# Gates of a product-key expert layer: summed and scattered into DRAM arrays instead of built by one-hot matmuls

## The chip, the cores and the metric

The kernel runs on one core of one Trainium2 chip. The metric is the device time of one execution in microseconds (us); smaller is better. TensorE is called PE, VectorE DVE, ScalarE ACT, GpSimd POOL and SyncE SP, as in the profile.

## What is computed

One decoder layer over T = 256 tokens of D = 2048. A mixing block (two projections, two causal convolutions, layer norm) gives x1; then every token chooses experts by product keys:

```python
q = (x_tok @ w_q).reshape(t, PEER_HEADS, 2, D_HALF)          # 8 heads
s = jnp.einsum('thpc,hpnc->thpn', q, sub_keys)               # 2 x 128 scores a head
s1, i1 = lax.top_k(s[:, :, 0], 16);  s2, i2 = lax.top_k(s[:, :, 1], 16)
cand = (s1[..., :, None] + s2[..., None, :]).reshape(t, 8, 256)
top_s, ci = lax.top_k(cand, 16)
experts = e1 * N_KEYS + e2                                   # e1, e2 looked up by ci; 16384 experts
g = jax.nn.softmax(top_s, axis=-1)
act = jax.nn.gelu(jnp.einsum('td,thkd->thk', x_tok, peer_u[experts]))
out = jnp.einsum('thk,thkd->td', act * g, peer_v[experts])
x = layer_norm(ALPHA * x + out)
```

Each token has 8 x 16 = 128 selections (expert, gate); two heads may select the same expert, and then their gates add.

## The kernel before

The kernel does not gather experts for most tokens. It multiplies x1 with all 16384 rows of `peer_u` and then all of `peer_v`, and weights the activations by a gate matrix that is zero where a token did not select the expert. 192 of the 256 tokens (`TD`) go this dense way. For the last 64 tokens (`SPARSE`) the activations are stored to DRAM, and the selected rows of `peer_v` are gathered by indirect DMAs and added on DVE (`pick`).

**Units.** All weights stream through as units of 128 x 1024 f32 (512 KB): SP loads a unit into one of 4 `raw` slots (`load`, which waits until the low part of the unit 4 before it is made), ACT rounds it into a high part (`hi`, line 638, which waits until PE has finished the unit 4 before it), DVE subtracts to get a low part (`lo`, line 876), and PE multiplies with 3 products per block: high by high, high by low, low by high (lines 1470 to 1472). Of the units from `U_Q` to `U_ROUTED`, POOL makes the low part (line 563) because DVE is busy with the routing (top-k, decoding the chosen indices). Between these loads SP also copies `peer_v` into a layout with whole rows (`copy_unit`, `v_rows`).

**Up stage.** Tile c (0 to 127) holds the activations of 128 experts for 256 tokens: 2 units, 48 matmuls of 256 columns into bank c % 2. ACT applies gelu when the tile is done and writes tokens 0 to 191 into `hid[:, c, :]` and the other 64 into `stage`. In this text unit n of the up stage is `U_UP + n`; tile c is units 2c and 2c + 1. The engines run in the order in which their code is written, so a wait holds everything behind it on its engine. ACT's and DVE's loops over c do, in turn, the high and low part of units a little ahead of the tile, and whatever the stage adds.

**Gates.** When the selections are ready (`sel`: first index, second index, gate; line 1211), PE transposes them (`transpose_selections`, in tile `SEL_AT` = 13). From tile 16 on, every third tile, the gates of 8 tokens are made (`gate_batch`): DVE builds two one-hot tiles (lines 1243 to 1259), PE multiplies them in 8 matmuls of 256 columns in 16-bit types (line 1606) between the two units of a tile, ACT and DVE put the result (high and low part) into `hid` and `gtmp` and fold it into the activations already there. There are 24 batches; the last stands in tile 85. Later tiles are multiplied as they come (`gate_tile_of`, line 1279).

**Down stage.** `coef_hi` and `coef_lo` split 4 tiles of `hid` (a group g, 32 groups) into operands, and PE multiplies them with the units of `peer_v`. Then comes the last layer norm.

## Time and profile before

| | |
|---|---|
| median of 3 runs | 1789.7 us (1789.25 to 1790.16) |
| profiled execution | 1791.2 us |
| its span, first to last instruction | 1789.4 us |
| mean granted TensorE clock | 0.996 |
| PE, PE weight load, DVE, ACT, POOL busy | 98%, 90%, 75%, 48%, 26% |
| DMA | 534.5 MB moved, 299 GB/s |

A busy PE is not a PE at its peak: matmuls overlap, so their durations (about 280 ns each in the up stage) say little, and the distance from one start to the next says what one costs. Idle time of the other engines matters only where PE waits at the end of it.

### The profile page before, as it was taken

To read this page: it belongs to the slowest core of one execution; us is meant where nothing else is said; L and a number is where in the kernel's file an instruction comes from. 1 tells how busy PE (TensorE), PEld (TensorE's weight loads), DVE (VectorE), ACT (ScalarE), POOL (GpSimd) and SP (SyncE) were. 2 spreads that over 40 slices of the span, in tenths; PEclk is the share of its full clock that TensorE was granted. 3 is DMA by queue.
4 is the path that set the end of the run, shared out by engine and by line. 5 is a ranking of instruction groups with operands and counts; after the bars stand their busy time and mean duration, and the time that the engine had idled before them with its cause. 6 is when DMAs were issued, how large, how long until landed. Compare 5 with 4: busy or idle time off the path is not lost.

```text
span 1789.4 us, 31898 instructions
## 1 busy us (share of the span) xinstructions
PE 1761.0 (98%) x12082; PEld 1618.3 (90%) x12082; DVE 1338.9 (75%) x1897; ACT 853.5 (48%) x1208; POOL 467.1 (26%) x278
## 2 busy tenths in 40 slices
PE   7999999899999999999999999999999999999997
PEld 7999987799999999999999999988878788888875
DVE  7999997687847777777775444557888888888876
ACT  5544445444544444444444444444544445445544
POOL 0000000488850000000000000034568775454401
PEclk9999999999999999999999999999999999999999
DMA  7788878778888888878888888878999999999973
GB/s 265 283 306 292 290 271 292 276 275 269 290 285 282 278 274 277 281 266 281 276 274 290 292 288 292 294 231 310 366 382 374 387 384 377 358 368 350 344 254 119
DMA packets 184098, 534.50 MB, mean 299 GB/s; under 512 B 35344, under 2 KB 35472, under 8 KB 182416
## 3 DMA queue, kind: packets, MB, share of 16 engines
q1 hardware_dynamic: 149664, 460.64, 73.0%
q0 software_dynamic: 16464, 67.68, 10.0%
q10 hardware_dynamic: 17888, 5.26, 1.2%
q8 instruction: 30, 0.49, 0.1%
q14 instruction: 52, 0.43, 0.1%
HBM read 524.50 MB, written 109.05 MB: 354 GB/s over the span
## 4 chain that ended last, share of the span: by engine, by line
PE 95%; DVE 2%; issue 1%; DMA 1%; ACT 1%; DVEq 0%; POOLq 0%; POOL 0%; SPq 0%; ACTq 0%
PE psum L1470 19%; PE psum L1472 19%; PE psum L1471 19%; PE psum L1643 6%; PE psum L1639 6%; PE psum L1644 6%; PE psum L1641 6%; PE psum L1640 6%; PE psum L1606 1%; PE psum L1514 1%; PE psum L1516 1%; PE psum L1515 1%; DMA raw<-in_v_w_dram 1%; DVE w_lo L876 1%; PE psum L1554 0%
## 5 line engine op out<-in xcount | busy, mean ns | idle before, releaser
L638 ACT ACTIVATE w_hi<-raw 128x1024 fp32r<-128x1024 f32 x570 | 604.0, 1061 | 736.4 <-PE psum L1472 492.9
L1470 PE MATMUL psum<-xt_hi,w_hi 128*128 128x256 f32 x2944 | 827.5, 281 | 11.8 <-DVE xt_lo L890 9.4
L876 DVE TENSOR_TENSOR w_lo<-raw,w_hi 128x1024 fp32r<-128x1024 f32 x506 | 614.1, 1223 | 292.2 <-ACT w_hi L638 281.1
L1471 PE MATMUL psum<-xt_lo,w_hi 128*128 128x256 f32 x2944 | 823.7, 280 | 0.0
L1472 PE MATMUL psum<-xt_hi,w_lo 128*128 128x256 f32 x2944 | 823.5, 280 | 0.0
L1470 PEld LDWEIGHTS psum<-xt_hi,w_hi 128*128 128x128 f32 x2944 | 555.5, 189 | 12.4 <-issue 12.0
L1471 PEld LDWEIGHTS psum<-xt_lo,w_hi 128*128 128x128 f32 x2944 | 555.4, 189 | 0.0
L1472 PEld LDWEIGHTS psum<-xt_hi,w_lo 128*128 128x128 f32 x2944 | 555.3, 189 | 0.0
L586 POOL DMA_INDIRECT rows<-v_rows,sp_idx x64 | 112.2, 1754 | 767.8 <-DMA v_rows<-in_v_w_dram 621.1
L563 POOL TENSOR_TENSOR w_lo<-raw,w_hi 128x1024 fp32r<-128x1024 f32 x64 | 153.8, 2408 | 363.2 <-ACT w_hi L638 363.1
L1639 PE MATMUL psum<-w_hi,c_hi 128*128 128x512 f32 x504 | 199.6, 396 | 0.9 <-DVE w_lo L876 0.8
L1641 PE MATMUL psum<-w_hi,c_lo 128*128 128x512 f32 x504 | 199.3, 396 | 0.0
L1640 PE MATMUL psum<-w_lo,c_hi 128*128 128x512 f32 x504 | 199.3, 395 | 0.0
L1644 PE MATMUL psum<-w_lo,c_both 128*128 128x512 f32 x504 | 199.3, 395 | 0.0
L1643 PE MATMUL psum<-w_hi,c_both 128*128 128x512 f32 x504 | 199.3, 395 | 0.0
L1342 DVE SCALAR_TENSOR_TENSOR picked<-rows,sp_coef,picked 128x2048 f32<-128x2048 f32 x63 | 148.1, 2351 | 0.5 <-DMA rows<-in_v_w_dram,sp_idx 0.4
L638 ACT ACTIVATE w_hi<-raw_late 128x1024 fp32r<-128x1024 f32 x82 | 87.0, 1062 | 96.4 <-PE psum L1644 85.2
L1639 PEld LDWEIGHTS psum<-w_hi,c_hi 128*128 128x128 f32 x504 | 94.7, 188 | 25.1 <-DVE w_lo L876 2.2
L1643 PEld LDWEIGHTS psum<-w_hi,c_both 128*128 128x128 f32 x504 | 94.7, 188 | 23.1 <-DVE w_lo L876 0.2
L1641 PEld LDWEIGHTS psum<-w_hi,c_lo 128*128 128x128 f32 x504 | 94.7, 188 | 22.9
L1644 PEld LDWEIGHTS psum<-w_lo,c_both 128*128 128x128 f32 x504 | 94.7, 188 | 22.9
L1640 PEld LDWEIGHTS psum<-w_lo,c_hi 128*128 128x128 f32 x504 | 94.7, 188 | 22.6
(191 smaller groups left out, 1395.9 us busy)
## 6 DMA issues: line engine op xcount, KB each, us to landing
raw<-in_u_w_dram SPq DMA_DIRECT2D x256, 512.0 KB
v_rows<-in_v_w_dram SPq DMA_DIRECT2D x192, 512.0 KB, 5.3
raw<-in_v_w_dram SPq DMA_DIRECT2D x172, 512.0 KB
raw_late<-in_v_w_dram SPq DMA_DIRECT2D x84, 512.0 KB
raw<-in_w_in_dram SPq DMA_DIRECT2D x80, 512.0 KB
raw<-in_w_out_dram SPq DMA_DIRECT2D x32, 512.0 KB
raw<-in_w_q_dram SPq DMA_DIRECT2D x32, 512.0 KB
act_spill<-stage ACTq DMA_DIRECT2D x32, 128.0 KB, 4.4
```

The source lines that it names most:

```text
L563: nc.gpsimd.tensor_tensor(w_lo[s][:, :], raw[:, s, :], w_hi[s][:, :].bitcast(f32), ALU.subtract).then_inc(lo_done[s], SPLIT)
L638: nc.scalar.activation(parts_of(slot_u)[0][:, :], raw_of(slot_u), ACT.Copy).then_inc(hi_done, 1)
L876: tt(lo_w[:, :], raw_of(slot_u), hi_w[:, :].bitcast(f32), ALU.subtract).then_inc(lo_done[slot_u % SPLIT], SPLIT)
L1342: i = stt(picked[:, :], rows[k % ROWS][:, :], sp_coef[:, k:k + 1], picked[:, :], ALU.mult, ALU.add)
L1470: mm(dst, hi_w[:, sl], xt_hi[:, kk, :], start=st, stop=False)
L1471: mm(dst, hi_w[:, sl], xt_lo[:, kk, :], start=False, stop=False)
L1472: i = mm(dst, lo_w[:, sl], xt_hi[:, kk, :], start=False, stop=en)
L1639: mm(v_bank(j, 0), hi_c[:, n, :], w1, start=st, stop=False)
L1640: mm(v_bank(j, 0), hi_c[:, n, :], w2, start=False, stop=False)
L1641: i = mm(v_bank(j, 0), lo_c[:, n, :], w1, start=False, stop=en)
L1643: mm(v_bank(j, 1), both_c[:, n, :], w1, start=st, stop=False)
L1644: i = mm(v_bank(j, 1), both_c[:, n, :], w2, start=False, stop=en)
```

## The change

No one-hot tiles, no gate matmuls and no transposes of the selections. Instead:

- DVE computes an id (e1 * 128 + e2) for each selection and, for every selection of a token, the sum of the gates of all selections of that token with the same id (`merge`: compare, multiply, reduce over 128 x 8 x 128 elements at a time). `merge(0)` does tokens 0 to 127 in 16 rounds; `merge(1)` does tokens 128 to 191, spread over all 128 partitions, in 8 rounds. ACT issues the DMAs that lay the inputs and the results out (`SEL_AT` = 10, `RELAY0_AT` = 20, `RELAY1_AT` = 26).
- SP writes zeros into 6 DRAM arrays of 2 MB, 32 tokens each (`zeros`, 8 times 6 DMAs of 256 KB, units 16 to 72 of the whole stream).
- POOL scatters the sums into the arrays with 32 x 6 = 192 indirect DMAs of 128 elements of 4 bytes; each waits for the one before it on its array. Equal selections write equal sums.
- SP loads the gates of a group of 4 tiles with 6 DMAs of 64 KB (`gates`), the first before unit 195 of the up stage; DVE multiplies them into `hid` (`gate_group`), from its loop step c = `GATED_AT` = 95 on, ahead of the low part of unit 2c + 3.
- POOL makes 16 more low parts (`U_ROUTED` = `U_UP` + 48 instead of 32), and the copies of `peer_v` end 48 units sooner (`COPY1`).

The core of the diff ("..." where lines are left out):

```diff
-PART_OF_TILE = 6
+PART_OF_TILE = 2
-SEL_AT = 13
-U_ROUTED = U_UP + 32
-GATE0 = 16
-GATE_STEP = 3
+SEL_AT = 10
+ROUTED_AT = 30
+U_ROUTED = U_UP + 48
+GATED_AT = 95
+RELAY0_AT, RELAY1_AT = 20, 26
+SAME = 8
+TOKENS = 32
+ZEROED = 4
+ARRAYS = TD // TOKENS
+QUARTERS = P // TOKENS
+EACH = SELECTED // QUARTERS
+def gates_unit(g):
+    return U_UP + 2 * (GATED_AT + g - 2) + 9
-COPY0, COPY1 = 24, U_DOWN - 8
+COPY0, COPY1 = 24, U_UP + 200
...
@@ sync
+            def zeros(n):
+                if n == 0:
+                    sp.wait_ge(zero_made, 1)
+                for a in range(ARRAYS):
+                    sp.dma_start(gate_tiles[a][:, ZEROED * n:ZEROED * (n + 1), :],
+                                 g_buf[:, 0, 0:ZEROED].rearrange("p g k t -> p g (k t)")).then_inc(zero_out, 16)
+            def gates(g):
+                if g == 0:
+                    for done in scattered:
+                        sp.wait_ge(done, 16 * EACH)
+                if g >= 2:
+                    sp.wait_ge(gated_done, g - 1)
+                for a in range(ARRAYS):
+                    sp.dma_start(g_buf[:, g % 2, a].rearrange("p k t -> p (k t)"), gate_tiles[a][:, g, :])\
+                        .then_inc(g_in[g % 2], 16)
             def stream(src, base, first, end):
                 for n in range(first, end):
                     u = base + n
+                    if 16 <= u < 16 + 8 * GROUPS // ZEROED and u % 8 == 0:
+                        zeros((u - 16) // 8)
+                    for g in range(GROUPS):
+                        if u == gates_unit(g):
+                            gates(g)
                     load(u, src[n])
...
@@ gpsimd
+            pool.wait_ge(zero_out, 16 * ARRAYS * GROUPS // ZEROED)
+            pool.wait_ge(relaid, 16 * ARRAYS * QUARTERS)
+            for k in range(EACH):
+                for a in range(ARRAYS):
+                    if k:
+                        pool.wait_ge(scattered[a], 16 * k)
+                    nc.gpsimd.indirect_dma_start(
+                        gate_array[a], bass.IndirectOffsetOnAxis(sc[:, a, 1, k:k + 1].bitcast(u32), 0),
+                        sc[:, a, 0, k:k + 1], None).then_inc(scattered[a], 16)
...
@@ scalar
-            def gates_out(m):
...
+                if c == RELAY0_AT:
+                    act.wait_ge(scat_ready, 1)
+                    for a in range(P // TOKENS):
+                        for q in range(QUARTERS):
+                            act.dma_start(sc[TOKENS * q:TOKENS * (q + 1), a, :, :],
+                                          sums[0][TOKENS * a:TOKENS * (a + 1), :, EACH * q:EACH * (q + 1)])\
+                                .then_inc(relaid, 16)
+                if c == RELAY1_AT:
+                    act.wait_ge(scat_ready, 2)
...
@@ vector
+            def merge(part, own, everyone, gates, n):
+                link_dup(nc.vector.tensor_copy(all_ids[part], everyone))
+                dve.wait_ge(dup, n_dup[0])
+                link_dup(ts(place_f[part][:, :], own, float(TOKENS), tok[:, 1:2], ALU.mult, ALU.add))
+                dve.wait_ge(dup, n_dup[0])
+                link_dup(nc.vector.tensor_copy(sums[part][:, 1, :].bitcast(u32), place_f[part][:, :]))
+                def matches(m):
+                    link_dup(tt(same[m % 2], own[:, SAME * m:SAME * (m + 1)].unsqueeze(2).to_broadcast([P, SAME, SELECTED]),
+                                all_ids[part].unsqueeze(1).to_broadcast([P, SAME, SELECTED]), ALU.is_equal))
+                matches(0)
+                for m in range(n // SAME):
+                    dve.wait_ge(dup, n_dup[0])
+                    link_dup(tt(same[m % 2], same[m % 2], gates.unsqueeze(1).to_broadcast([P, SAME, SELECTED]), ALU.mult))
+                    product = n_dup[0]
+                    if m + 1 < n // SAME:
+                        matches(m + 1)
+                    dve.wait_ge(dup, product)
+                    i = nc.vector.tensor_reduce(sums[part][:, 0, SAME * m:SAME * (m + 1)], same[m % 2], AX.X, ALU.add)
...
+            def gate_group(g):
+                dve.wait_ge(gelu_done, PART_OF_TILE * GROUP * (g + 1))
+                dve.wait_ge(g_in[g % 2], 16 * ARRAYS * (g // 2 + 1))
+                mine = hid[:, GROUP * g:GROUP * (g + 1), :].rearrange("p k (a t) -> p a k t", a=ARRAYS)
+                tt(mine, mine, g_buf[:, g % 2], ALU.mult).then_inc(gated_done, 1)
...
             for c in range((U_ROUTED - LEAD - U_UP) // 2, N_KEYS):
                 u = U_UP + 2 * c + LEAD
+                if c >= GATED_AT and c - GATED_AT < GROUPS - 1:
+                    gate_group(c - GATED_AT)
+                for v in (u, u + 1):
+                    if v >= U_ROUTED:
+                        lo(v, v)
...
@@ tensor
-            def gate_batch(m):
-                pe.wait_ge(oh1_done, m + 1)
-                pe.wait_ge(oh2_done, PARTS * m + PARTS)
...
-                for t in range(BATCH):
-                    i = mm(bank[2 + t // 2][:, (t % 2) * PARTS * N_KEYS:(t % 2 + 1) * PARTS * N_KEYS], oh1[:, t // INNER, :, t % INNER],
-                           oh2g[:, t // INNER, :, :, t % INNER].rearrange("p w e -> p (w e)"), start=True, stop=True)
-                i.then_inc(g_done, 1)
```

On DVE, behind the last instruction of the routing (it makes the gates in `sel`), the kernel before goes on with PE's transposes and the first one-hots, and then with the low parts:

```order
L1211 TENSOR_TENSOR sel<-sel,ssum 128x256 [waits rt]
L1214 CAST tab<-psum 128x256 [waits sel_tr]
L1216 TENSOR_SCALAR gate_e<-gate 128x256 [waits tabs_copied]
...
L1243 TENSOR_TENSOR oh<-iota_t,tab 128x1024 [waits tabs_copied,tabs_done]
L1245 TENSOR_TENSOR oh<-oh,gate_p 128x1024 [waits oh1_eq]
L1251 TENSOR_TENSOR oh2g<-iota_t,tab 128x4x256
L1259 TENSOR_TENSOR oh2g<-oh2g,gate_t 128x4x256 [waits oh2_eq]
L1259 TENSOR_TENSOR oh2g<-oh2g,gate_t 128x4x256 [waits oh2_done]
L876 TENSOR_TENSOR w_lo<-raw,w_hi 128x1024 [waits hi_done] x5
```

In the changed kernel the same place reads as follows (the three lines 1277, 1283 and 1288 come 24 times in all, and 903 is the low part):

```order
L1238 TENSOR_TENSOR sel<-sel,ssum 128x256 [waits rt]
...
L1270 COPY psum<-ids 128x128 [waits sel_done,dup]
L1272 TENSOR_SCALAR place_f<-ids,tok 128x128 [waits dup]
L1274 CAST sums<-place_f 128x128 [waits dup]
L1277 TENSOR_TENSOR psum<-ids,psum 128x1024
L1283 TENSOR_TENSOR psum<-psum,sel 128x1024 [waits dup]
L1277 TENSOR_TENSOR psum<-ids,psum 128x1024
L1288 TENSOR_REDUCE sums<-psum 128x8 [waits dup]
...
L1288 TENSOR_REDUCE sums<-psum 128x8 [waits dup]
L903 TENSOR_TENSOR w_lo<-raw,w_hi 128x1024 [waits hi_done,dup]
```

The first low part that DVE makes itself (of unit 48) now stands behind all 24 rounds.

On SP, the loads around unit 195 of the up stage, before:

```order
L481 DMA v_rows<-in_v_w_dram 128x2x512
L464 DMA raw<-in_u_w_dram 128x1024 [waits lo_done1]
L464 DMA raw<-in_u_w_dram 128x1024 [waits lo_done2]
L481 DMA v_rows<-in_v_w_dram 128x2x512
L464 DMA raw<-in_u_w_dram 128x1024 [waits lo_done3]
```

and in the changed kernel:

```order
L476 DMA v_rows<-in_v_w_dram 128x2x512
L459 DMA raw<-in_u_w_dram 128x1024 [waits lo_done2]
L476 DMA v_rows<-in_v_w_dram 128x2x512
L500 DMA g_buf<-gate_spill 128x128 [waits scattered3,scattered4,scattered2,scattered5,scattered1,scattered0]
L500 DMA g_buf<-gate_spill 128x128 x5
L459 DMA raw<-in_u_w_dram 128x1024 [waits lo_done3]
```

The six loads of gates stand between the loads of units 194 and 195, and the first of them waits for the end of all scatters.

On DVE, the low parts of the up stage in the changed kernel, up to unit 192 and on from 193:

```order
L1353 MEMSET stats 128x1 [waits idx_done,scat_ready]
L903 TENSOR_TENSOR w_lo<-raw,w_hi 128x1024 [waits hi_done] x138
L1304 TENSOR_TENSOR hid<-hid,g_buf 128x6x4x32 [waits g_in0,gelu_done]
L903 TENSOR_TENSOR w_lo<-raw,w_hi 128x1024 [waits hi_done] x2
L1304 TENSOR_TENSOR hid<-hid,g_buf 128x6x4x32 [waits g_in1,gelu_done]
L903 TENSOR_TENSOR w_lo<-raw,w_hi 128x1024 [waits hi_done] x2
```

The first product with gates stands ahead of the low part of unit 193 and waits for the six loads.

## Rows read from the trace of the kernel before

**Rows 1.** The page: busy time by engine; PE's granted clock in 40 slices.

```profile
PE 1761.0 (98%) x12082; PEld 1618.3 (90%) x12082; DVE 1338.9 (75%) x1897; ACT 853.5 (48%) x1208; POOL 467.1 (26%) x278
...
PEclk9999999999999999999999999999999999999999
```

**Rows 2.** The page: the chain that ended last, by engine.

```profile
PE 95%; DVE 2%; issue 1%; DMA 1%; ACT 1%; DVEq 0%; POOLq 0%; POOL 0%; SPq 0%; ACTq 0%
```

**Rows 3.** Timeline of PE (start, length, operation): one gate batch.

```profile
530.41 0.28 PE L1472 MATMUL psum<-xt_hi,w_lo 128*128 128x256 f32 x1
530.53 1.08 PE L1606 MATMUL psum<-oh2g,oh 128*128 128x256 f16 x8
...
531.57 0.28 PE L1471 MATMUL psum<-xt_lo,w_hi 128*128 128x256 f32 x1
```

**Rows 4.** Groups by line: count | busy, mean ns | idle before.

```profile
L1606 PE MATMUL psum<-oh2g,oh 128*128 128x256 f16 x192 | 26.0, 277 | 0.0
```

**Rows 5.** The chain in order of time: start, length, what.

```profile
513.23 0.66 PE psum L1595 x6
```

**Rows 6.** Timeline of ACT: high parts in tiles 12 and 13; a DMA issue.

```profile
504.92 1.06 ACT L638 ACTIVATE w_hi<-raw 128x1024 fp32r<-128x1024 f32 x1 [1.74 <-PE psum L1472]
...
510.52 1.06 ACT L638 ACTIVATE w_hi<-raw 128x1024 fp32r<-128x1024 f32 x1 [1.74 <-PE psum L1472]
...
529.41 0.38 ACTq L763 DMA_DIRECT2D act_spill<-stage  x1
```

**Rows 7.** Timeline of DVE: two rounds of the decoding, and what follows.

```profile
475.82 1.23 DVE L1198 TENSOR_TENSOR psum<-psum,hidx_f 128x1024 f32<-128x1024 f32 x1
...
479.34 1.23 DVE L1198 TENSOR_TENSOR psum<-psum,hidx_f 128x1024 f32<-128x1024 f32 x1
...
482.48 1.12 DVE L1211 TENSOR_TENSOR sel<-sel,ssum 128x256 f32<-128x256 f32 x1
...
514.69 2.38 DVE L1216 TENSOR_SCALAR gate_e<-gate 128x256 uint32<-128x256 uint32 x1 [0.34 <-ACT gate L804]
517.00 0.28 DVE L1218 TENSOR_SCALAR gate_m<-gate 128x256 uint32<-128x256 uint32 x1
```

**Rows 8.** Timeline of POOL: a low part, then its indirect DMAs.

```profile
514.53 2.40 POOL L563 TENSOR_TENSOR w_lo<-raw,w_hi 128x1024 fp32r<-128x1024 f32 x1 [0.42 <-ACT w_hi L638]
...
1141.65 1.17 POOL L586 DMA_INDIRECT rows<-v_rows,sp_idx  x1 [621.12 <-DMA v_rows<-in_v_w_dram]
...
1181.15 0.94 POOL L595 DMA_INDIRECT sp_act<-act_spill,sp_idx  x1 [34.27 <-DMA act_spill<-stage]
...
1183.68 1.97 POOL L595 DMA_INDIRECT sp_act<-act_spill,sp_idx  x1 [0.31 <-issue]
...
1196.17 0.94 POOL L595 DMA_INDIRECT sp_act<-act_spill,sp_idx  x1 [4.02 <-issue]
...
1210.39 0.94 POOL L595 DMA_INDIRECT sp_act<-act_spill,sp_idx  x1 [4.25 <-issue]
```

**Rows 9.** Timeline of DVE in the same stretch.

```profile
1182.47 2.36 DVE L876 TENSOR_TENSOR w_lo<-raw,w_hi 128x1024 fp32r<-128x1024 f32 x2
```

**Rows 10.** The page: DMA issues, count, KB each, median us to landing.

```profile
v_rows<-in_v_w_dram SPq DMA_DIRECT2D x192, 512.0 KB, 5.3
...
act_spill<-stage ACTq DMA_DIRECT2D x32, 128.0 KB, 4.4
```

**Rows 11.** Windows: PE, PEld, DVE, ACT, POOL busy, PEclk, DMA share, GB/s.

```profile
112.00:134.00 22.00, 22.00 (x191) 22.00 (x190) 22.00 (x33) 9.29 (x10) 0.00 (x0) 1.00 0.91 324
...
335.00:340.00 5.00, 2.76 (x13) 2.79 (x14) 5.00 (x9) 0.49 (x1) 0.67 (x1) 0.50 0.87 299
...
1062.00:1178.00 116.00, 116.00 (x993) 115.81 (x992) 56.80 (x65) 51.69 (x84) 4.32 (x4) 1.00 0.82 279
```

**Rows 12.** Timeline of PE behind a wait: a unit's first matmul, the next work.

```profile
337.24 0.55 PE L1470 MATMUL psum<-xt_hi,w_hi 128*128 128x256 f32 x1 [2.38 <-issue]
...
342.20 1.47 PE L1540 MATMUL psum<-ident,acc 128*128 128x128 f32 x12
```

More of the change, by code:

```diff
@@ L76 @@
 U_LAST = U_DOWN + 2 * NCH * G_LAST
-def gate_tile(m):
-    return GATE0 + GATE_STEP * m
-def gated_tokens(c):
-    return BATCH * len([m for m in range(NB) if gate_tile(m) <= c])
+def gates_unit(g):
+    return U_UP + 2 * (GATED_AT + g - 2) + 9
 def coef_slot(g):
@@ L299, in build @@
         act_tiles = act_dram.rearrange("(c p t) o -> p c (t o)", c=N_KEYS, p=P, t=SPARSE)
+        gate_array = [nc.dram_tensor(f"gate_spill{a}", [P * N_KEYS * TOKENS, 1], f32, kind="Internal").ap()
+                      for a in range(ARRAYS)]
+        gate_tiles = [x.rearrange("(p g c) o -> p g (c o)", p=P, g=GROUPS, c=GROUP * TOKENS) for x in gate_array]
         v_rows = nc.dram_tensor("v_rows", [N_KEYS * N_KEYS, JOINED * DCH], f32, kind="Internal").ap()
@@ L1275, in gate_tile_of, with link_dup, flat @@
-            def gate_tile_of(c):
-                n = gated_tokens(c)
-                dve.wait_ge(gelu_done, PART_OF_TILE * (c + 1))
-                tt(hid[:, c, 0:n], bank[6 + c % 2][:, 0:n], hid[:, c, 0:n], ALU.mult).then_inc(hid_done, 1)
+            n_dup = [0]
+            def link_dup(ins):
+                n_dup[0] += 1
+                ins.then_inc(dup, 1)
+            def flat(x):
+                return x.rearrange("p h k -> p (h k)")
+            dve.wait_ge(rt, R[0])
+            for b in range(TB):
+                i = stt(ids[:, b], flat(sel[:, 0, b]), float(N_KEYS), flat(sel[:, 1, b]), ALU.mult, ALU.add)
+                if b == TB - 1:
+                    i.then_inc(id_done, 1)
+                else:
+                    link_dup(i)
@@ L1401, in _ @@
                 if u == U_DOWN:
[L1402 removed]
+                    gate_group(GROUPS - 1)
                 if u in coef_at:
```

252 lines of the change are left out of this document (75 added, 177 removed).

## The prediction

> **What bounds the kernel now.** I read busy time and chain first. PE is busy 98% of the span at full clock [rows 1] and makes up 95% of the chain that ended last [rows 2]. So time goes away only where PE issues less, and is added only where PE waits. Next I read, stage by stage, whether PE really never waits: in 1062 to 1178 us it is busy for all 116 us, while DVE is busy for 56.8, ACT for 51.7 and POOL for 4.3 [rows 11]. The gate batches stand inside this PE stream, so I looked at one from both sides [rows 3]. Last I needed the pace without gates: the same high part (ACT's second in a tile, which starts when PE has ended the tile) starts at 504.92 and 510.52 us [rows 6], so a tile takes 5.60 us, a unit 2.80 and a matmul of 256 columns 5.60 / 48 = 0.117 us. The second of these starts marks the end of tile 12. Without gates, tile c ends at 510.5 + 5.6 (c - 12).
>
> **What goes away on PE.** From the start of the batch to the second matmul behind it pass 531.57 - 530.53 = 1.04 us [rows 3]; without the batch it would be one matmul, 0.12. A batch costs 0.92 us, not the 277 ns x 8 of its row. There are 192 / 8 = 24 [rows 4], which is 22.1 us, and the six transposes cost 0.66 [rows 5], altogether **22.7 us** off. The one-hots and folds leave DVE and ACT, which were not waited for: no time, but DVE is then free for what follows.
>
> **The routing gets longer.** DVE ends the old routing at 482.48 + 1.12 = 483.6 us [rows 7]. Now 24 rounds follow at once. Each has the three operations, operand places (one in PSUM) and sizes of a round of the decoding, and such rounds start 479.34 - 475.82 = 3.52 us apart [rows 7]: 24 x 3.52 = 84.5 us. Ahead of the rounds stand some 10 small operations. Alone they cost about 0.3 us each, but an operation on SBUF waits for a POOL operation on SBUF that has begun: the same kind takes 2.38 us beside POOL's low part of 514.53 to 516.93, and 0.28 just behind it [rows 7, 8]. So the ten cost 3 us at the least and 14 at the most; I take 9.5, since POOL is busy for 2.4 of each 2.8 us. DVE ends at 577.6 (571 to 582). Unit 48 is the first whose low part is again DVE's (1.2 us, half of the pair in [rows 9]), so PE can start it at 578.8. It wants it when tile 23 has ended, at 510.5 + 5.6 x 11 = 572.1. **PE waits 6.7 us** (0 to 11). POOL's 16 more low parts hide: 2.40 us each [rows 8] at a pace of 2.80. Queued behind the late low part on DVE are those of units 49 to 54 and the selections of the sparse tokens; their users come later by the same shift.
>
> A wait has a price behind it. After PE's waits around 335 us its granted clock was 0.50, the lower of its two levels, 1.2 GHz [rows 11], and the first unit afterwards (24 matmuls, 337.24 to 342.20) took 4.96 us instead of 2.80 [rows 12]. I add **2.2 us**: the routing costs 8.9 in all.
>
> ACT's DMA issues are 8 in tile 10, 16 in tile 20 and 8 in tile 26. One takes about 0.38 us [rows 6], 16 take 6.1. They stand between ACT's high parts; a high part starts 8.4 us (3 units) before PE wants the unit, and needs 1.1 us itself and 2.4 on POOL, so 4.9 us hide. The 16 may hold PE for 1 to 2 us, but this comes out of the wait at unit 48, whose end is set by DVE. Nothing is added.
>
> **Zeros.** 12.6 MB are written within units 16 to 72, some 160 us, or 79 GB/s. DMA carries 324 GB/s there already at a share of 0.91 [rows 11], and the copies get denser (192 in 320 units, not 368: 15 GB/s more). 324 / 0.91 is 356 GB/s, so the sum of 418 would overflow for parts of this stretch; but most of it carries less, and the 0.91 holds copies and bias loads. PE's cushion is about the 4.9 us of slack above, and DVE has none here (22 busy of 22 us). Bounds: 0, if the bursts fit between the peaks, and 6.7, if each of the six bursts under copies (1.57 MB, 4.4 us at 356 GB/s) eats 2 us more than DVE can make up and PE's cushion hides 5. I take **1 us**, near the lower end, since PE waits for no load in this stretch before.
>
> **The scatter and its deadline.** This decides the sign. Unit 48 starts at 578.8; unit 52 is over 5 x 2.8 + 2.2 later, at 595.0. Then ACT makes a high part (1.06), issues its last 8 DMAs (3.0), and they land 4.4 to 5.3 us later [rows 6, 10]: POOL starts to scatter at about 604. PE wants unit 193 at 578.8 + 2.2 + 145 x 2.8 = 987.0. Back from there: the low part 1.2, the product with gates about 1.0 (768 columns against 1024 in 1.2), landing of the gates 5.3, six issues 2.3, landing of the last scatter 4.4 [rows 6, 9, 10], in all 14.2. The last scatter must be issued by 972.8, so 192 scatters have 369 us, **1.92 us each**.
>
> No scatter stands in the trace; the nearest rows are the gathers of the same size. Fourteen of them, 1181.15 to 1210.39, took 29.2 us, 2.09 each, and in this are two pauses of 4.02 and 4.25 us, each after seven in a row [rows 8]. With the pauses 192 take 401 us; without them 29.2 - 8.3 + 0.6 over 14 is 1.54, so 296 us. The rows give no reason for the pauses but that seven had gone out with no wait between them. A scatter waits for the sixth one before it on its array, so there are never more than six open. I take 1.54, which ends at 900, far in time: no cost. Both ends go into the range.
>
> Here a rule of the Trainium skill can be weighed. The row: a gather lasts 0.94 us alone and 1.97 when it starts inside DVE's low parts of 1182.47 to 1184.83 [rows 8, 9]. The Trainium skill ("SBUF — State Buffer", Who interferes with whom) says that a DVE `tensor_tensor` was not seen to stall descriptor writing, and infers that it leaves the interface free that this needs. By the row a scatter costs 1.54 us among DVE's low parts, by the rule 0.94 + 0.30 = 1.24, so 238 us; the trace contradicts the rule, and either is below the limit.
>
> **Gates in.** 32 times 6 loads of 512 B pieces, 12.6 MB in 180 us, 70 GB/s more, while the copies (about 98 GB/s) end at unit 200: DMA stays under its 0.82 [rows 11] or near it. Steady state: the loads are issued after low part +4 of their group and wanted after +6, 5.6 us later; issue and landing take 7.6. DVE waits some 2 us a group and multiplies for 1.0, within the 4.9 that hide. If that cover went, each group would cost PE up to 3 us.
>
> **Sum.** Against the profiled execution of 1791.2 us: 1791.2 - 22.7 + 6.7 + 2.2 + 1.0 = 1778.4. The median of the runs is 1.5 lower than the profiled one, so 1777 us; that is 0.7% faster.
>
> **Rivals.**
> - The scatter is late (slower). The pauses come back, since they could belong to the number issued and not to the number open. 401 us end 32 us after the deadline; SP stands before the load of unit 195 and DVE before the low part of 193, PE waits 32, plus 2.2 for the clock: 1811. It decides at 1.92 us a scatter, and at 2.02 (pauses, but less of DVE than at 1181) it is 19 late: 1798. Chance 0.24.
> - A little late: pauses half as long give 1.8 to 1.95; PE waits up to 6 and pays the 2.2: 1777 to 1785. Chance 0.10.
> - Routing and zeros both at their upper ends: 11 instead of 6.7 and 6.7 instead of 1, so 1787. For it: DVE saturated in the first stage. Chance 0.10.
> - The batches were hidden: then nothing goes away, and 1797 or so remains. Against it: PE has no gap around them and starts are 0.92 apart. Chance 0.02.
> - DVE's routing ends before unit 48 is wanted: no wait, 1768. It needs small operations that hardly meet POOL. Chance 0.09.
> - The forecast as summed, 1771 to 1783: 0.45.
>
> **How the numbers follow.** Two tenths of a per cent, 3.6 us, is about what a measurement of this kernel can tell from no change. Faster than 1786.1: the forecast, the early routing, nearly all of the little-late case and half of the case of upper ends, 0.67, less a little for steps I have missed: 0.64. Slower than 1793.3: the late scatter and the hidden batches, 0.25. The same: 0.11. The range leaves out half of the early routing below and the worst late scatters above: 1768 to 1802.
>
> **What would show it.** PE: no rows of 16-bit matmuls, tiles 5.60 us apart from 12 to 95. DVE: 24 rounds 3.52 apart, end near 578; a PE gap of some 7 us before unit 48 and clock 0.5 behind it. POOL: scatter starts near 604, and the distance of its rows settles the main doubt: 1.5 or 2.0. SP: whether the first load of gates waits for a scatter. If PE has a gap near 990, the forecast is wrong at the pace of the scatters; if DVE waits for loads between 80 and 220 us, at the zeros.

## The result, and the profile after

The changed kernel takes **2030.6 us** (median of 4 runs, 2028.8 to 2035.6) against 1789.9 before (1789.3 to 1791.1): a ratio of **1.135, 95% interval 1.133 to 1.137**. The forecast was 1777, in a range of 1768 to 1802. The profiled execution took 2035.6 us with a span of 2033.6; the one of before took 1791.2.

The page shows where. Busy time and instructions by engine; then PE, POOL, PE's granted clock and GB/s in 40 slices of 50.8 us:

```profile
PE 1782.5 (88%) x11884; PEld 1631.0 (80%) x11884; DVE 1287.0 (63%) x1686; ACT 824.6 (41%) x1089; POOL 679.8 (33%) x487
...
PE   8999998999997111159999999999999999999997
...
POOL 0000001788836777700000000000466666545401
PEclk9999998999997555579999999999999999999999
...
GB/s 272 351 355 359 323 266 335 275 280 306 306 269 181 11 24 1 11 156 304 297 306 303 299 306 324 288 265 247 267 350 378 389 399 374 362 350 376 368 251 133
...
PE 73%; issue 14%; DVE 4%; DMA 4%; SPq 2%; ACT 1%; DVEq 1%; ACTq 0%; POOLq 0%; POOL 0%
```

Before, PE was at 98% with its clock at 9 throughout [rows 1], and the chain was PE for 95% [rows 2]. Now PE is nearly idle for some five slices, 632 to 888 us, at the lower clock; in the last line, the chain by engine, "issue" has come from 1% to 14%. "Issue" is time in which the engine waited for nothing that the profile shows. These are just the slices in which POOL issues the scatters. The same stretch in windows (columns as in [rows 11]):

```profile
618.00:631.00 13.00, 13.00 (x113) 13.00 (x112) 4.94 (x4) 4.58 (x8) 10.26 (x10) 1.00 1.00 364
632.00:640.00 8.00, 5.25 (x20) 4.05 (x21) 1.23 (x1) 1.06 (x1) 6.47 (x6) 0.69 0.33 112
700.00:740.00 40.00, 5.49 (x15) 4.03 (x14) 0.00 (x0) 0.00 (x0) 30.24 (x33) 0.50 0.02 0
...
1062.00:1178.00 116.00, 116.00 (x988) 116.00 (x987) 50.28 (x41) 50.50 (x84) 0.00 (x0) 1.00 0.88 303
```

For 13 us PE and the scatters run side by side. Then PE starves, and with it everything: in 700 to 740 us DVE and ACT have nothing to do and DMA moves nothing. It looks as if loads were missing. The timelines say otherwise. POOL:

```profile
617.76 1.20 POOL L626 DMA_INDIRECT gate_spill<-sc  x1 [33.12 <-DMA sc<-sums]
...
702.08 0.96 POOL L626 DMA_INDIRECT gate_spill<-sc  x1 [0.30 <-issue]
703.34 0.96 POOL L626 DMA_INDIRECT gate_spill<-sc  x1 [0.30 <-issue]
...
863.07 0.95 POOL L626 DMA_INDIRECT gate_spill<-sc  x1 [0.31 <-issue]
```

PE, at the onset, in the middle and at the end, and one weight load of the middle:

```profile
631.65 0.28 PE L1484 MATMUL psum<-xt_hi,w_hi 128*128 128x256 f32 x1
632.73 0.29 PE L1485 MATMUL psum<-xt_lo,w_hi 128*128 128x256 f32 x1 [0.80 <-issue]
...
700.54 0.37 PE L1486 MATMUL psum<-xt_hi,w_lo 128*128 128x256 f32 x1 [2.43 <-issue]
703.34 0.37 PE L1484 MATMUL psum<-xt_hi,w_hi 128*128 128x256 f32 x1 [2.43 <-issue]
...
699.14 0.29 PEld L1486 LDWEIGHTS psum<-xt_hi,w_lo 128*128 128x128 f32 x1 [2.51 <-issue]
...
887.62 0.57 PE L1484 MATMUL psum<-xt_hi,w_hi 128*128 128x256 f32 x1 [0.33 <-issue]
888.30 0.37 PE L1485 MATMUL psum<-xt_lo,w_hi 128*128 128x256 f32 x1
```

Inside one unit, whose weights have all arrived, PE issues **one matmul every 2.80 us**: with the weight load 1.40 us ahead of each, 1.40 us an instruction. 24 such matmuls are 67 us, which is why ACT's high parts stand some 66 us apart there; the loads are late because nobody frees their buffers. The stall begins 14 us, ten scatters, after the first one and ends 25 us after the last. POOL does not slow in this run: nearly all of its scatters start 1.26 us apart. Nor do the scatters queue up as DMAs: in the stall the last of a scatter's 32 packets is moved 1.72 us after its start in the median and 4.3 at the most, and the last packet of all at 865 us, 23 us before PE recovers.

To place the rest I took the start of the same unit's high part in both profiled executions. The units are counted here from the start of the whole stream, in which the up stage begins at 144. The changed kernel is later by 5.9 us at unit 16, though only by 0.9 at unit 23, and by 13.1 at unit 120 (end of the first stages); 11.5 at unit 184 and 15.9 at unit 200 (routing); 16.0 at unit 207 and **257.2** at unit 216 (the stall, 241 us); 243.4 at unit 320 (batches gone), 245.1 at 360 (gates in), 244.1 at the end. So the stall explains 241 of 244 us; without it gains and losses would about cancel. Of the losses the zeros are the largest. SP's queue, what ACT's high parts waited for, and what PE waited for in the first 260 us:

```profile
39.53 0.44 SPq L517 DMA_DIRECT2D acc<-in_x_nat_dram  x1
40.01 2.87 SPq L489 DMA_DIRECT2D gate_spill<-g_buf  x6
```

```profile
ACT w_hi L668 <- DMA raw<-in_w_in_dram: 90.7, 50, 7.5
```

```profile
PE psum L1484 <- DVE w_lo L903: 8.4, 8, 4.1
```

The first burst of zeros goes out right behind the 2 MB of x_nat. ACT waits 90.7 us for loads in the first stages, in 50 places (the three numbers are the sum, the count and the longest wait); before it was 5.9 in 6. PE feels it through the low part: it waits for DVE 8 times, 8.4 us in all, and before it waited for no low part here.

The routing, on DVE, ACT and PE:

```profile
580.60 1.23 DVE L1283 TENSOR_TENSOR psum<-psum,d_gates 128x1024 f32<-128x1024 f32 x1
...
584.12 1.23 DVE L1283 TENSOR_TENSOR psum<-psum,d_gates 128x1024 f32<-128x1024 f32 x1
...
586.53 2.45 DVE L903 TENSOR_TENSOR w_lo<-raw,w_hi 128x1024 fp32r<-128x1024 f32 x2
```

```profile
565.65 10.63 ACTq L830 DMA_DIRECT2D sc<-sums  x16
576.38 1.06 ACT L668 ACTIVATE w_hi<-raw 128x1024 fp32r<-128x1024 f32 x1 [9.70 <-issue]
...
577.90 0.57 PE L1484 MATMUL psum<-xt_hi,w_hi 128*128 128x256 f32 x1 [3.98 <-ACT hid L780]
```

The rounds are 3.52 us apart as forecast, and DVE ends at 586.5, 575 without the 11.5 us by which it was late. But PE does not wait for DVE. It waits 4.0 us for a gelu that stands behind ACT's sixteen DMA issues, which take 0.66 us each and not 0.38.

### The profile page after: what moved, and what is told of

It is laid out like the page before. It is cut to its first block, busy times and chain, and to the rows that moved or that the text cites. A ratio compares the mean times of both kernels' runs of the same rounds, so it can differ in the third digit from the quotient of the medians.

```text
span 2033.6 us, 31494 instructions
## 1 busy us (share of the span) xinstructions
PE 1782.5 (88%) x11884; PEld 1631.0 (80%) x11884; DVE 1287.0 (63%) x1686; ACT 824.6 (41%) x1089; POOL 679.8 (33%) x487
## 4 chain that ended last, share of the span: by engine, by line
PE 73%; issue 14%; DVE 4%; DMA 4%; SPq 2%; ACT 1%; DVEq 1%; ACTq 0%; POOLq 0%; POOL 0%
PE psum L1484 14%; PE psum L1485 14%; PE psum L1486 14%; PE psum L1622 6%; PE psum L1618 6%; PE psum L1623 6%; PE psum L1620 6%; PE psum L1619 6%; DMA raw<-in_w_in_dram 3%; DVE w_lo L903 1%; DVE cacc L942 1%; PE psum L1528 1%; PE psum L1530 1%; PE psum L1529 1%; SPq L489 1%
## 5 line engine op out<-in xcount | busy, mean ns | idle before, releaser
L903 DVE TENSOR_TENSOR w_lo<-raw,w_hi 128x1024 fp32r<-128x1024 f32 x490 | 593.1, 1221 | 575.7 <-ACT w_hi L668 445.4
L1486 PE MATMUL psum<-xt_hi,w_lo 128*128 128x256 f32 x2944 | 832.1, 283 | 77.9 <-issue 77.8
L1485 PE MATMUL psum<-xt_lo,w_hi 128*128 128x256 f32 x2944 | 832.5, 283 | 70.4 <-issue 70.2
L1484 PEld LDWEIGHTS psum<-xt_hi,w_hi 128*128 128x128 f32 x2944 | 562.5, 191 | 98.2 <-issue 86.8
L1486 PEld LDWEIGHTS psum<-xt_hi,w_lo 128*128 128x128 f32 x2944 | 562.4, 191 | 84.5 <-issue 84.3
L1485 PEld LDWEIGHTS psum<-xt_lo,w_hi 128*128 128x128 f32 x2944 | 562.4, 191 | 66.2 <-issue 66.1
L583 POOL TENSOR_TENSOR w_lo<-raw,w_hi 128x1024 fp32r<-128x1024 f32 x80 | 192.0, 2410 | 388.1 <-ACT w_hi L668 387.9
L606 POOL DMA_INDIRECT rows<-v_rows,sp_idx x64 | 104.0, 1624 | 550.2 <-DMA v_rows<-in_v_w_dram 389.6
L626 POOL DMA_INDIRECT gate_spill<-sc x192 | 188.0, 979 | 91.4 <-issue 58.2
L615 POOL DMA_INDIRECT sp_act<-act_spill,sp_idx x64 | 88.3, 1380 | 206.0 <-DMA act_spill<-stage 167.8
```

Source lines behind the costliest of these rows:

```text
L583: nc.gpsimd.tensor_tensor(w_lo[s][:, :], raw[:, s, :], w_hi[s][:, :].bitcast(f32), ALU.subtract).then_inc(lo_done[s], SPLIT)
L626: nc.gpsimd.indirect_dma_start(gate_array[a], bass.IndirectOffsetOnAxis(sc[:, a, 1, k:k + 1].bitcast(u32), 0), sc[:, a, 0, k:k + 1], None) ...
L903: tt(lo_w[:, :], raw_of(slot_u), hi_w[:, :].bitcast(f32), ALU.subtract).then_inc(lo_done[slot_u % SPLIT], SPLIT)
L1484: mm(dst, hi_w[:, sl], xt_hi[:, kk, :], start=st, stop=False)
L1485: mm(dst, hi_w[:, sl], xt_lo[:, kk, :], start=False, stop=False)
L1486: i = mm(dst, lo_w[:, sl], xt_hi[:, kk, :], start=False, stop=en)
```

## The experiments

Theory at the start: the scatters, and only they, stall PE. Rivals: PE is slow there by itself (its loop, the supply of its instructions); writes to DRAM back up; or it is the issuing of indirect DMAs. That POOL is merely busy is no rival: with low parts alone it is busy for 2.40 of each 2.80 us in the same kernel, with PE at its full pace. Each edit is against the changed kernel unless another is named.

**The scatters out.**

```diff
-            for k in range(EACH):
-                for a in range(ARRAYS):
...
-                    nc.gpsimd.indirect_dma_start(gate_array[a], ..., sc[:, a, 0, k:k + 1], None)
```

The loads of gates wait for the zeros instead of the scatters.

> All 192 scatters are left out (the gates stay zero, so the output is not the reference's); zero writes, merging of equal selections, relays, the loads of gates and the products with them all stay. In the trace of the changed kernel the same unit's high part is 16.0 us later than before at unit 208 of the stream and 257.1 us later at unit 216, and in between TensorE issues one matmul every 2.80 us with no wait that the trace names, from 14 us after the first scatter to 20 us after the last. Theory A (the scatters cause this stretch and nothing else does): 2030.6 - 241 = 1790 us, between 1786 and 1794. Theory B (TensorE is slow there for another reason, for instance its own loop or the zero writes): over 1900 us. Either way the rows ahead of unit 208 stay as they are: 13 us late at the end of the first stages, 16 at unit 208.

Measured: 1786.4 us, ratio 0.9975 (0.9964 to 0.9986). No stall. It is 7.1 us late at unit 120 and 5.1 early at the end. Part of what the batches give back is lost again: from the routing to the loads of gates a tile takes 5.65 us here, as in the changed kernel, and not the 5.60 of before, nearly 4 us in some 75 tiles, with PE busy throughout. No run shows why; where a trace has both paces, the change comes where PE has stopped for a moment.

**Gathers instead of scatters.**

```diff
-                        gate_array[a], bass.IndirectOffsetOnAxis(sc[:, a, 1, k:k + 1].bitcast(u32), 0),
-                        sc[:, a, 0, k:k + 1], None)
+                        sc[:, a, 0, k:k + 1], None, gate_array[a],
+                        bass.IndirectOffsetOnAxis(sc[:, a, 1, k:k + 1].bitcast(u32), 0))
```

> Each of the 192 scatters is replaced by a gather with the same indices, the same array in DRAM and the same waits, 128 elements of 4 bytes read from DRAM into the place in SBUF from which they were written (so the gates that are multiplied in stay zero and the output is not the reference's). Theory A (small writes to DRAM back up, and TensorE is slowed behind them): no slow stretch, 1790 us like the kernel without scatters. Theory B (it is the back-to-back issuing of indirect DMAs by GpSimd, in whichever direction): a matmul every 2.8 us again and 1950 to 2035 us.

Measured: 2031.7 us, 1.134 (1.132 to 1.137). The same stall, a matmul every 2.80 us. Writing gates to DRAM is not needed for it; theory A of this run fell.

**The scatters paced.**

```diff
             for k in range(EACH):
+                pool.wait_ge(hi_done, U_UP + 62 + 4 * k)
```

> The scatters are all made, but six at a time: the k-th six wait for the high part of unit 62 + 4k of the up stage, so six go out (7.6 us at 1.265) in every 11.2 us. Theory A (something fills while scatters are issued and empties in the pauses: TensorE began to stall 14 us after the first scatter and recovered 20 us after the last): a six fits into the 14 us and is followed by 3.6 us of rest, so the stall is shorter or gone: 1785 to 1850 us. Theory B (every scatter delays TensorE by a share of its own 1.265 us): the same 241 us in smaller pieces, 1990 to 2040 us.

Measured: **1788.3 us**, 0.9988 (0.9978 to 0.9997). One line takes the stall away. The 320 us around the scatters, of this kernel:

```profile
603.00:923.00 320.00, 319.20 (x2719) 318.81 (x2718) 138.44 (x113) 138.86 (x228) 194.36 (x163) 1.00 0.89 303
```

and of the changed kernel:

```profile
603.00:923.00 320.00, 109.16 (x659) 98.29 (x659) 35.83 (x44) 33.59 (x56) 188.04 (x192) 0.60 0.23 73
```

POOL is busy for about as long in both, with scatters alone (163 and 192 of them). PE is busy for 319 us or for 109. The scatters cost PE next to nothing when six are followed by a pause of 2.2 to 2.5 us: it stopped at "issue" twice, for 0.4 us each, at 736 and 918 us, which the kernel without scatters does not.

**PE's loop written out.**

```diff
-            with pe.Fori(1, N_KEYS // 2) as i:
-                for r in range(2):
-                    up(2 * i + r, r)
+            for c in range(2, N_KEYS):
+                up(c, c)
```

> Only TensorE's loop over the tiles of the up stage is written out in full, nothing else is changed. In the slow stretch the trace shows TensorE idle with no wait before each matmul, so its instructions may come late. Theory A (it is something behind the engine that all of its instructions meet): as the changed kernel, 2020 to 2040 us. Theory C (the loop's instructions are fetched again at each jump back and the scatters hold up this fetch): with no jumps the slow stretch changes strongly, to below 1900 us or, if straight code fetches more, above 2100 us.

Measured: 2033.1 us, 1.135 (1.132 to 1.139). The jumps of the loop have no part in it. Nor was the supply of instructions held up as far as the traces show it: with PE's loop written out the DMA queue that carries 16 KB blocks of instructions moved one about every 15 us at full pace and, in the stall, one in over 200 us, as few as PE's slow progress needs; in the changed kernel it moved none there.

**Copies late** (paced kernel).

```diff
-COPY0, COPY1 = 24, U_UP + 200
+COPY0, COPY1 = 80, U_UP + 200
```

> The paced kernel, with the copies of v_w to v_rows starting at unit 80 instead of 24 (same end, so denser behind 80). The paced kernel is 6.0 us later than before at unit 16, right after the first burst of zeros (six DMAs behind the 2 MB load of x_nat), and 7.1 to 11.5 later from unit 48 on; DMA's share in 80 to 140 us is 1.02 at 389 GB/s, against 0.90 at 320 before. Theory A (zeros and copies together overflow DMA; the zeros alone would fit, but for the first burst): the 6 us at unit 16 stay, the rest up to unit 120 goes: 1782 to 1785 us. Theory B (the bursts of zeros cost their 4.4 us each whatever runs beside them): 1788 us again, 7 to 11.5 us late from unit 48 on.

Measured: 1784.1 us, 0.9967 (0.9957 to 0.9977); 5.9 us late at unit 16, 1.4 at 63, 2.5 at 120, against 6.0, 2.9 and 8.9 of the paced kernel. In 80 to 140 us DMA's share is 0.80 at 279 GB/s, against 1.02 at 389. Zeros and copies together overflow DMA. Zeros alone cost little: each burst holds up a high part by 3 to 6 us, the first one too, and nearly all of it is made up before the next.

**Zeros spread** (paced kernel): one write of 256 KB just ahead of each load of units 144 to 191. `zero_one` issues one of the six DMAs of `zeros`.

```diff
-                    if 16 <= u < 16 + 8 * GROUPS // ZEROED and u % 8 == 0:
-                        zeros((u - 16) // 8)
+                    if U_UP <= u < U_UP + ARRAYS * GROUPS // ZEROED:
+                        zero_one(*divmod(u - U_UP, ARRAYS))
```

> The paced kernel, with the 48 zero writes (256 KB each) one at a time, one behind each load of units 144 to 191, instead of six at a time at every eighth unit from 16 to 64. There DVE and TensorE's loads have slack (DVE busy for 37.8 of 50 us in 400 to 450 us, DMA share 0.81 at 279 GB/s; 256 KB per 2.8 us are 94 GB/s more, together 373, near the 389 seen at share 1.02). Theory A (the delay of the first stages is the zeros'): 0 to 1 us late at unit 120 instead of 11.2, and 1777 us, or up to 1782 if the fuller stretch behind costs some. Theory B (it is the denser copies or DVE): still 8 to 11 us late at unit 120, 1786 to 1790 us.

Measured: **1778.7 us**, 0.9938 (0.9920 to 0.9956); 0.5 us early at unit 120 where the paced kernel was 8.9 late. The denser stretch behind it (450 to 500 us at 398 GB/s) cost PE nothing: it was busy for all 50 us.

**Runs of 24** (paced kernel, the same mean rate as long as PE keeps its pace).

```diff
-                pool.wait_ge(hi_done, U_UP + 62 + 4 * k)
+                if k % 4 == 0:
+                    pool.wait_ge(hi_done, U_UP + 62 + 4 * k)
```

> As the paced kernel, with the same number of scatters in the same time, but 24 in a row (30 to 36 us) for every 44.8 us instead of 6 in a row for every 11.2. Theory A (what counts is how long the run is: TensorE stalled from 14 us, 12 scatters, after the first one on): the second half of every burst stalls TensorE, 8 bursts of 12 scatters, 15 us each, and some 20 us behind each: 1900 to 2030 us. Theory B (the mean rate decides, 68% of the time is below what it takes): 1788 us like the paced kernel.

Measured: 1935.7 us, 1.081 (1.079 to 1.084). Seven of the eight runs stall PE, from 11 to 18 us after their first scatter until about 4 us after their last, and each makes PE some 18 us later; the eighth brings four short pauses. The waits follow PE's progress, so with the stalls the mean became 2.57 us a scatter, slower than the 1.87 of the paced kernel, and still it stalls. The length of a run matters, not only the mean.

**Half the elements, and an eighth.**

```diff
-                        gate_array[a], bass.IndirectOffsetOnAxis(sc[:, a, 1, ...
-                        sc[:, a, 0, k:k + 1], None)
+                        gate_array[a], bass.IndirectOffsetOnAxis(sc[0:64, a, 1, ...
+                        sc[0:64, a, 0, k:k + 1], None)
```

> The changed kernel with no pacing, but each of the 192 scatters covers 64 partitions instead of 128 (half of the gates are never scattered, so the output is not the reference's). Theory A (a backlog of single elements: 24576 of them in 245 us are more than is drained, half of them are not): no stall, 1788 to 1795 us, if an issue takes as long as before. Theory B (a cost of every indirect instruction, whatever its size): a matmul every 2.8 us again, 1950 to 2035 us. If an issue takes half as long, the number of elements per us stays the same, and theory A expects a stall of half the length, about 1910 us.

> The changed kernel with no pacing, but each of the 192 scatters covers 16 partitions instead of 128, so one element of 4 bytes or so for each DMA engine (seven eighths of the gates are never scattered, so the output is not the reference's). Scatters of 64 stalled TensorE exactly as those of 128 did (2034 and 2031 us). Theory A (a cost of every indirect DMA, whatever it carries): the same stall while they are issued, 1950 to 2035 us, a little shorter if an issue gets shorter. Theory B (elements count, and 64 are simply still too many): no stall, 1786 to 1795 us.

Measured: 2034.4 us, 1.136 (1.134 to 1.139), with 64 elements and 2033.8, 1.135 (1.133 to 1.138), with 16 (the same edit with `0:16`). An issue takes 0.90 and 0.83 us instead of 0.96, and the stall is as long, 258 and 260 us against 257. It goes with the number of DMAs, not with how many elements they carry; the packets in the trace are 32 a scatter in both the full and the smallest form, so their number is not separated from that of the DMAs. With the shorter issue the scatters should end sooner, but POOL falls into PE's step. With 16 elements nearly all start 1.14 us apart up to the 115th, and from there on mostly 1.40:

```profile
743.98 0.84 POOL L626 DMA_INDIRECT gate_spill<-sc  x1 [0.30 <-issue]
...
750.22 1.09 POOL L626 DMA_INDIRECT gate_spill<-sc  x1 [0.30 <-issue]
751.62 1.09 POOL L626 DMA_INDIRECT gate_spill<-sc  x1 [0.30 <-issue]
```

With 64 the same begins at about the 160th. So in the end POOL's scatters and PE's instructions both go one in 1.40 us. One thing that both need, that serves one in this time and holds a backlog of limited size, would look like this; that is argued, not shown.

**Direct DMAs of POOL** in place of the indirect ones.

```diff
-                    nc.gpsimd.indirect_dma_start(gate_array[a], ..., sc[:, a, 0, k:k + 1], None)
+                    nc.gpsimd.dma_start(gate_array[a][P * k:P * (k + 1), :], sc[:, a, 0, k:k + 1])
```

> The changed kernel without pacing, with each indirect scatter replaced by a direct DMA issued by GpSimd, of the same 128 times 4 bytes into the same array at fixed rows (the gates land in the wrong places, so the output is not the reference's). Gathers, scatters and scatters of half the size all stalled TensorE, with 0.90 to 0.96 us and 0.30 of pause for each. Theory A (any DMA that GpSimd describes in software does it when issued back to back for over 11 us): a stall again, 1950 to 2040 us if an issue takes 1.2 us as well. Theory B (only the indirect form): 1788 to 1795 us.

Measured: 2263.3 us, 1.263 (1.259 to 1.267), but by another cause, so it decides nothing. The group of these DMAs, the share of DMA, and what PE waited for:

```profile
gate_spill<-sc POOLq DMA_DIRECT2D x192, 0.5 KB, 21.7
```

```profile
700.00:800.00 100.00, 48.22 (x300) 47.03 (x300) 14.61 (x12) 14.57 (x24) 14.59 (x27) 0.71 1.04 106
```

```profile
PE psum L1483 <- ACT hid L779: 375.4, 42, 18.6
```

A column of 128 times 4 bytes took 21.7 us to land, and DMA was full at 106 GB/s. POOL waited for landings and issued one in 3.7 us, and PE waited for late tiles and hardly at "issue" (2.3 us, once). Whether direct DMAs back to back would stall PE is not answered.

**Relays spread** (kernel with spread zeros).

```diff
-                if c == RELAY0_AT:
+                if RELAY0_AT <= c < RELAY0_AT + P // TOKENS:
                     act.wait_ge(scat_ready, 1)
-                    for a in range(P // TOKENS):
+                    for a in [c - RELAY0_AT]:
...
```

The eight relays at `RELAY1_AT` are spread in the same way.

> The kernel with paced scatters and spread zeros, with ACT's relay DMAs issued four a tile (tiles 20 to 23, 26 and 27) instead of 16 in tile 20 and 8 in tile 26. In the run with spread zeros these 16 took 10.6 us on ACT, and TensorE waited 4.0 us at 560 to 564 us for the gelu behind them; DVE ended the merging at 575.6 us, just in time for the delayed TensorE. Theory A (two waits lie side by side: without ACT's, TensorE reaches unit 48 at about 572 and waits there 4 us for DVE's low part instead): as before, 1777 to 1780 us. Theory B (ACT's issues were the only wait): 1772 to 1775 us.

Measured: 1778.8 us, 0.9924 (0.9901 to 0.9946), the same as without it. ACT's wait of 4.0 us was gone, and PE waited for DVE instead, as theory A has it (waits in 540 to 620 us):

```profile
PE psum L1485 <- DVE w_lo L904: 2.8, 1, 2.8
```

The two waits differ in what followed. The granted clock is the last but two of these columns; the first row is of the kernel with spread zeros alone, behind its wait of 4.0 us for ACT, the second of this one, behind its wait of 2.8 us for DVE:

```profile
564.00:575.00 11.00, 10.71 (x70) 10.72 (x71) 10.86 (x10) 4.83 (x9) 7.04 (x3) 0.74 0.65 223
```

```profile
576.00:587.00 11.00, 10.42 (x89) 10.43 (x90) 6.87 (x7) 3.51 (x5) 0.00 (x0) 1.00 0.90 323
```

So in the traces this stretch got 4 us cheaper, although the medians are equal; the profiled execution lost 2 us in the first stages, where the edit changes nothing. Whether the other executions lost the rest in the same way is not shown.

**Relays spread and DVE's low parts eight units later.**

```diff
-ROUTED_AT = 30
-U_ROUTED = U_UP + 48
+ROUTED_AT = 34
+U_ROUTED = U_UP + 56
```

> As the kernel with relays spread, and GpSimd keeps the low parts for eight units more (to unit 55 of the up stage instead of 47), so that DVE has 22.4 us more before its first low part is wanted; the selections of the sparse tokens move by one tile with it. Theory A (with both waits gone TensorE has no gap at all between 500 and 620 us; 4.0 us of wait and about 2 of the slower clock behind it): 1771 to 1774 us. Theory B (GpSimd's extra low parts and later scatters cost elsewhere, the gates come late near 990 us): 1777 us or more.

Measured: **1771.6 us**, 0.9879 (0.9857 to 0.9902), the fastest: 1.2% under before. In these windows PE has no gap at the routing, and hardly one in the 320 us of scatters:

```profile
560.00:616.00 56.00, 56.00 (x482) 56.00 (x481) 31.59 (x41) 24.43 (x40) 32.59 (x18) 1.00 0.91 313
```

```profile
603.00:923.00 320.00, 319.85 (x2728) 319.65 (x2727) 141.13 (x129) 139.46 (x228) 204.72 (x173) 1.00 0.90 305
```

**Faster paces**: two scatters a unit (on the kernel with spread zeros; the wait stands before every second scatter, for the high part of unit 66 + 3k + a // 2), and six for 3.5 units (on the fastest one; this edit is shown).

```diff
-                pool.wait_ge(hi_done, U_UP + 62 + 4 * k)
+                pool.wait_ge(hi_done, U_UP + 62 + 7 * k // 2)
```

> The kernel with paced scatters and spread zeros, but two scatters for every unit of 2.80 us (1.40 us each on the average) instead of six for every four (1.87 us each), so there is hardly a pause. Runs of 24 at 1.32 us each stalled TensorE after 11 to 17 us; six at 1.4 us with 2.2 to 2.5 us of pause never did. Theory A (what fills empties only in pauses of microseconds): a stall of the length of after, 1900 us or more. Theory B (it drains at about one for 1.3 us, so 1.40 is just slow enough): 1779 us as with the slower pace.

> The fastest version so far (relays spread, DVE's low parts from unit 56 on, 1771.6 us), with six scatters for every 3.5 units instead of every 4: 1.63 us each on the average instead of 1.87, against 1.40 that cost about 43 us. A six takes about 8.4 us, so 1.4 us of pause are left in 9.8. Theory A (any pause that lets the mean fall below some 1.5 us is enough): 1770 to 1774 us, as before. Theory B (it needs the pause of over 2 us): stalls of some us in many of the 32 rounds, 1780 to 1800 us.

Measured: 1821.8 us, 1.016 (1.013 to 1.019), at 1.40 us a scatter, so 43 more than at 1.87; and 1797.0, 1.002 (1.001 to 1.004), at 1.63, so 25 more. Both theories of the first run were too simple: there are a dozen short stalls of 1 to 7 us at 1.40, and nine at 1.63. These paces are those that the waits set while PE keeps its own; each stall of PE stretches them, and the scatters came one in 1.64 and 1.81 us on the mean. PE's waits in the second of the runs:

```profile
PE psum L1485 <- issue: 7.3, 13, 2.4
PE psum L1486 <- issue: 6.9, 13, 0.9
```

The first pace that costs next to nothing lies between 1.63 and 1.87 us a scatter, as the waits set it, not far from the one that I had chosen.

## Why the prediction was wrong

- **The step that failed** is the one that sets the sign: "I take 1.54, which ends at 900, far in time: no cost." The price on POOL was right enough (1.26 us while DVE is idle, up to 1.89 beside its low parts), the deadline was kept, and the cost was 241 us. I had asked only whether the scatters would be late, and taken an issue on POOL to be free for every other engine if its data is small. The runs show that a long series of POOL's indirect DMAs slows PE's own instructions to one in 1.40 us: no scatters, no stall; gathers, fewer elements or straight code on PE, the same stall; the same scatters with pauses, none to speak of.
- The rows of before could hardly warn of it. In [rows 8] fourteen gathers go out in two sevens with pauses of over 4 us, and PE is busy throughout (the window in [rows 11] ends before them; this one has them):

```profile
1181.00:1211.00 30.00, 30.00 (x130) 24.18 (x129) 17.69 (x17) 15.12 (x17) 17.92 (x15) 1.00 0.77 260
```

  I took these rows as a price for 192 without a pause and argued only over what the pauses would add. They stood for a pattern that never runs for longer than 11 us.
- The rivals missed it as well: both slow cases put the wait at unit 193, near 990 us. It came at 632, with POOL on time.
- **Zeros**: forecast 1 us, measured 13.1 in the profiled execution of the changed kernel and 7.1 without scatters; the eight traces with the zeros in this place have 7 to 13. The upper bound of 6.7 was too low. My argument "PE waits for no load in this stretch before" holds for before only. The mechanism was the named one, zeros on top of denser copies, at places where the sum passes what DMA carries; moved to where DVE has slack, they cost nothing. What was mis-sized is how much of a burst is made up: with the copies off behind the same bursts 2.5 us stay, with them 7 to 13. The changed kernel is 1 us late at unit 23, 3 at 39, 9 at 63 and 13 at 80.
- **Routing**: forecast 8.9 us, measured 7.2. The changed kernel loses 4.4 us from unit 184 to 200, and in the same stretch the kernel before pays for three batches, 2.8 us, that the changed one has not. The rounds are right at 3.52. The wait was put on DVE, and it was ACT's: "this comes out of the wait at unit 48" was right about the overlap, but its size was taken from one issue of 0.38 us where a relay issue takes 0.66. The experiments show two waits side by side, 4.0 us for ACT and 2.8 for DVE: taking away ACT's changed nothing in the median, taking away both gave 7 us. By the same count of the traces the routing costs 6.7 us with spread zeros, 3.0 with the relays spread too, and nothing with the later low parts. The wait of 4.0 us and the slower clock behind it (2.2 us by [rows 12]) make 6.2 of the 6.7. The price that I had put behind a wait was not paid behind that of 2.8 us, where the clock stayed at 1.00.
- **Gates in**: forecast hidden, measured 1.7 us between units 320 and 360. DVE waited for the loads about as foreseen in the mean (1.6 us against 2), but for up to 7.2:

```profile
DVE hid L1304 <- DMA g_buf<-gate_spill: 44.9, 28, 7.2
```

- **Batches**: 22.7 us forecast. With pacing and spread zeros the end of a tile moves from 1.9 us late (tile 27) to 15.0 early (tile 85), 16.9 us for the 20 batches that stood there, where 0.92 us each makes 18.4; two pauses of PE beside the scatters, with the slower instructions around them, took 1.6 of these back. At the end the profiled execution is 13.6 early, where my sum had 12.8. So the price of a batch is confirmed, and the sum fits a kernel with two faults mended, which takes 1778.7 us against a forecast of 1777. That it fits to a microsecond or two is luck in part: the routing cost 2 us less and the zeros 1 us less than forecast, against 3 us beside the scatters and at the gates that the sum did not have.
- The rule that I weighed: a scatter of the paced kernel that starts just behind the start of a low part of DVE takes 1.89 us. Of its 192 scatters, 88 start while an instruction of DVE has over 0.3 us to go, and these take 1.21 to 1.90 us and end 0.8 to 1.1 us after that instruction; the other 104 take 0.95 to 1.00. By these rows a scatter's issue waits for the end of the DVE instruction that it finds running. POOL and DVE:

```profile
627.11 1.89 POOL L627 DMA_INDIRECT gate_spill<-sc  x1 [2.45 <-ACT w_hi L669]
629.30 0.96 POOL L627 DMA_INDIRECT gate_spill<-sc  x1 [0.31 <-issue]
```

```profile
626.94 1.23 DVE L904 TENSOR_TENSOR w_lo<-raw,w_hi 128x1024 fp32r<-128x1024 f32 x1 [1.11 <-ACT w_hi L669]
```

  The Trainium skill ("SBUF — State Buffer", Who interferes with whom) has not seen `tensor_tensor` stall descriptor writing. These rows speak against it once more, and the measurement decides.

## What to carry to other kernels

Price a new stream of DMAs on GpSimd not only by its own end but by what it does to the others, and look whether the rows that you price it from run for as long and as densely as the new one will. When you compare the same unit in two traces, add back what else the stretch has lost or gained: here three batches hid over a third of what the routing cost. If a trace shows an engine idle at "issue" before every instruction while loads have also stopped, read the instructions one by one first: here the loads were late because PE was, and not the reverse. A stream that has slack is best paced by the progress of the engine that must not wait, and each such move costs one wait on a semaphore. Measure a few paces before you trust one: here 1.87 us a scatter was nearly free, and 1.63 cost 25 us.

## What the runs showed of the hardware

- Indirect DMAs issued by GpSimd back to back (0.83 to 0.96 us and 0.30 of pause, 16 to 128 elements, gather or scatter) bring TensorE to 1.40 us an instruction. It starts 11 to 18 us after the first of a run and ends about 4 us after 24 of them and 25 to 28 us after 192, so something fills up and empties. Six in 11.2 us made PE pause for 0.7 us at the most, twice in 360 us.
- DVE's and ACT's next instructions started as soon as their inputs were there; they issue far fewer. GpSimd's own scatters, where their issue was short enough (0.83 and 0.90 us), fell to one in 1.40 us as well, after 115 and 160 of them.
- What it is that fills stays open. The instruction loop, the writes of gates to DRAM and the number of elements are excluded by experiments, and a queue of the scatters' own data by the trace (moved 1.72 us after the start of each in the median, 4.3 at the most). Semaphore updates, whatever else GpSimd does to issue a DMA, and the recording of the profile are not: each run whose time stands here also recorded its clock, so none tells whether the stall needs the recording. Nor was any form but the indirect one run back to back.
- In the paced kernel a scatter whose issue begins while a DVE instruction has over 0.3 us to go ends 0.8 to 1.1 us after that instruction (88 of 88), and takes 0.95 to 1.00 us otherwise (104 of 104).
- Over the 11 us around the end of a wait of 4.0 us TensorE's granted clock was 0.74 in the mean, around that of one of 2.8 us it was 1.00.
- ACT's DMA issue of a relay (32 partitions by 256 bytes) takes 0.66 us, that of a 128 KB spill 0.38.
- DMA carried 389 to 398 GB/s at a share of 1.02 to 1.03, above the 356 that I had worked out from [rows 11].
